# Setup of a fused layer kernel: token groups of 384, 384 and 264 in place of two of 512 and a patch, and ten identity products ahead of the first turn

## Chip, cores and metric

The kernel is one launch on one core of one Trainium2 chip. The metric is the device time of a launch in microseconds. Three runs of the kernel before gave 1665.57, 1666.29 and 1668.97 us, so the median is 1666.29 us.

## What is computed

One hybrid layer for a prompt of 1024 tokens and 8 decode tokens (1032 in all, model width 1024). What matters here is its head:

```
h    = rms_norm(x, norm_w)
proj = h @ w_in + b_in          # 1024 -> about 9,700 columns
```

The columns of `proj` then feed four branches (a gated delta rule, an RG-LRU, forgetting attention and attention to a memory), which are gated, merged and projected again. All of that is unchanged.

## The kernel before, in words

`h` is wanted transposed, with the model width on the partitions: `hH` and `hL` are [128, 8, 1032], a rounded high part and the rest, because every product of the projection is made of three passes (high weights by high `h`, high by low, low by high). A weight tile is 128 columns of `w_in`, split in the same way into `wH` (on ACT, L269, `split_hi`) and `wL` (on POOL, L276, `split_lo`). `project_step` (L335) makes one of the 8 k-steps of one tile for chosen groups of 344 tokens: three passes by up to three groups. A tile of three groups and 8 steps is 72 products. Its accumulators take three of the eight PSUM banks: tile 0 has banks 0 to 2, tile 1 has 3 to 5, and so on by turns, so that a group of a tile must not start in a bank that still holds something else.

`setup` (L357 to L586) makes `hH` and `hL` for all tokens, with tiles 0 and 1 projected in between:

- SP loads the 8 decode rows, then the 8 blocks of 128 token rows x_0 to x_7, with `norm_w` behind x_3 and the first weight tile behind x_5, then the second weight tile, then some twenty small parameter loads.
- ACT squares each block with a running sum (L448), DVE makes 1/sqrt of the sums by small dependent steps (`root`, L488 with L101 to L106, twice: for blocks 0 to 3, then for 4 to 7 and the decode rows), and the blocks are scaled by it: 0 to 3 on DVE (L494), 4 to 6 and the decode rows on ACT (L461, L465), 7 on POOL (L432).
- A "turn" (L526) is a set of PE transposes of one k of one token group into one PSUM bank, here 4 transposes of 128 columns. There are two groups of 512 tokens, so 16 turns. ACT writes the high part of a turned bank (`high`, L442), DVE the low part (`low`, L498), and the bank is free when the low part is there (`held`). The 8 decode tokens go their own way (L572, L514, L469, L518).
- PE first makes turns 0 to 5, which wait for all four scalings of DVE. Then `two_tiles` writes the order out by hand: tile 0, then tile 1, for the first 344 tokens (they need only the first token group), with the other ten turns between the steps; then tile 0 and tile 1 for the other two groups of 344, two at a time. The transposes of the parameter tables (`tables`, L531 to L536) stand behind the first step of the last loop.

The queues run in order: ACT has squares, splits, scalings and `high` in one written order, POOL has `split_lo` of tile 0, its scaling, then `split_lo` of tiles 1 and 2.

Behind it `conv_tiles` (L797) goes on with tile 2 on PE. Its own work hangs on setup's end in several chains. ACT rounds tile 2's weights once tile 0 is done, POOL makes their low part, then clears some buffers; DVE's convolution of tile 0 (L908 to L925) starts behind those, SP's loads of some narrow columns too, and SP's load of weight tile 3 stands behind these in its queue. PE's tile 3 needs tile 3's low weights, and behind its first step, before the squares' transposes (L781), it waits for the convolution of tile 0 (`fin`).

Of the kernel before, what the change touches and what calls it, by code (L numbers as in the profile page):

```python
# [356 lines left out]
def setup(K):  # L357

    nc, i, block = K.nc, K.i, K.block
    GROUPS = ((0, 1, 2, 3), (4, 5, 6, 7))  # L360
    TURNS = [(g, k) for g in range(2) for k in range(KD)]
    BANKS = [1, 2, 4, 5, 6, 7, 1, 2] + 2 * [4, 5, 6, 7]
    held = lambda x: max((y for y in range(x) if BANKS[y] == BANKS[x]), default=None)
    with ExitStack() as c:
# [4 lines left out]
        NW, HS = sb("norm_cols", [P, KD]), sb("h_sample", [P, KD, NB])  # L369
# [4 lines left out]
        made, squared, rstd = K.sem("constants_made"), K.sem("x_squared"), K.sem("x_rstd_made")  # L374
        by_act, by_dve, by_pool = (K.sem("x_scaled_" + x) for x in ("act", "dve", "pool"))
# [3 lines left out]
        sample, sampleT = K.sem("h_sample_steps"), K.sem("h_sample_turned")  # L379
# [20 lines left out]

        psum = lambda g, k: K.ps[:, BANKS[KD * g + k]]
        cols = lambda g: slice(512 * g, 512 * g + 512)
        HSP = K.ps[:, 1, 0:KD * NB]

        @block.sync
        def _(sp):
            sp.dma_start(X[0:NB, TT8], i["x_sample"][:, 0]).then_inc(x_in[TT8], 16)
            for t in range(TT8):
                sp.dma_start(X[:, t], i["x_prompt"][0, t * P:(t + 1) * P]).then_inc(x_in[t], 16)
                if t == 5:  # L410
                    K.loads(sp, 1)
                if t == 3:
                    sp.dma_start(NW[:], i["norm_w"][0].rearrange("(k p) -> p k", p=P),
                                 allow_slow_non_contiguous=True).then_inc(nw_in, 16)
            K.loads(sp, 2)
# [8 lines left out]
        def _(pool):  # L424
# [5 lines left out]
            K.split_lo(pool, 1)  # L430
            pool.wait_ge(rstd, 2)
            pool.tensor_scalar(X[:, 7], X[:, 7], RS[:, 7:8], None, ALU.mult).then_inc(by_pool, 1)  # L432
# [3 lines left out]
        def _(act):  # L436
# [7 lines left out]
            act.wait_ge(filled, 1)  # L444
            for x, t in enumerate((TT8, 0, 1, 2, 3, 4, 5, 6, 7)):
                n = P if t < TT8 else NB
                act.wait_ge(x_in[t], 16)
                act.activation(SQ[0:n], X[0:n, t], ACT.Square, accum_out=SS[0:n, t:t + 1]).then_inc(squared, 1)  # L448
                act.wait_ge(squared, x + 1)
                if t == 5:  # L450
                    K.split_hi(act, 1)
                    act.wait_ge(nw_in, 16)
                    high(0)
                    high(1)
                if t == 6:
                    high(2)
            for x in range(3, 6):
                high(x)
            act.wait_ge(rstd, 2)
            for t in (4, 5, 6):  # L460
                act.activation(X[:, t], X[:, t], ACT.Identity, scale=RS[:, t:t + 1]).then_inc(by_act, 1)  # L461
            high(6)
            high(7)
            K.split_hi(act, 2)
            act.activation(X[0:NB, TT8], X[0:NB, TT8], ACT.Identity, scale=RS[0:NB, TT8:TT8 + 1]).then_inc(by_act, 1)  # L465
            for x in range(8, 11):
                high(x)
            act.wait_ge(sample, 1)
            act.activation(K.hH[:, :, SEQ:TOK], HS[:], ACT.Identity).then_inc(sample, 1)  # L469
            for x in range(11, len(TURNS)):  # L470
                high(x)
# [12 lines left out]
        def _(dve):  # L484
            v = K.V(dve)

            def root(g, part):
# [4 lines left out]
            def scale(t):  # L492
                n = P if t < TT8 else NB
# [8 lines left out]
            dve.wait_ge(squared, 5)  # L502
            root(0, slice(0, 4))
            for t in range(4):
                scale(t)
            dve.wait_ge(nw_in, 16)
            for x, part in enumerate(TURNS):
                if x == 3:
                    dve.wait_ge(squared, 9)
                    root(1, slice(4, 9))  # L510
                low(*part)
                if x == 9:
                    dve.wait_ge(sampleT, 1)
                    dve.tensor_tensor(HS[:], HSP.rearrange("p (k b) -> p k b", b=NB),  # L514
                                      NW[:].unsqueeze(2).broadcast_to([P, KD, NB]), ALU.mult).then_inc(sample, 1)
                if x == 11:
                    dve.wait_ge(sample, 2)
# [2965 lines left out]
```

## Time and profile before

| | |
|---|---|
| runs | 1665.57, 1666.29, 1668.97 us |
| profiled execution | 1669.67 us, of which its span on the core 1668.0 us |
| mean granted TensorE clock | 0.995 |
| PE busy | 1612.3 us, 97% |
| DVE, ACT, POOL busy | 53%, 32%, 30% |

The profiled execution is one launch of its own; the span runs from its first to its last instruction. A time in the trace counts from the span's start. In a timeline row the columns are start, duration, engine, source line, operation, written<-read buffers, shapes (partitions x elements), how many instructions the row merges, and in brackets the idle time of the engine before it with what ended it.
### The profile page before, as it was taken

The numbers are of one execution on the slowest core, as the hardware profiler recorded it, in microseconds if no ns is written. First come the engines' busy times: TensorE is split into PE (matmuls) and PEld (weight loads), VectorE is DVE, ScalarE is ACT, GpSimd is POOL, SyncE is SP. The second block draws the span as 40 slices with busy tenths as digits, with TensorE's granted clock in tenths as the row PEclk, the third lists the DMA queues.
The fourth block names the chain that finished last, engine by engine and source line by source line (L and its number), as shares of the span: only waits on it lengthen the run. The fifth ranks groups of instructions, "written<-read, shape, count | busy, mean of one in ns | idle before, by whom it ended". The sixth has DMA issues, their size and how long they took to land. (4 is left out here: it accounts for less than half of the span.)

```text
span 1668.0 us, 26092 instructions
## 1 busy us (share of the span) xinstructions
PE 1612.3 (97%) x10579; PEld 1541.0 (92%) x10579; DVE 884.0 (53%) x1288; ACT 537.4 (32%) x934; POOL 502.6 (30%) x379
## 2 busy tenths in 40 slices
PE   5999999999999999999999999999999999999999
PEld 4989989999999999998889899999999999889976
DVE  4667853344444442790387672435657552995611
ACT  6323243222222222233334443321145223664200
POOL 2333415333343411911244551222212121103400
PEclk9999999999999999999999999999999999999999
DMA  4211155223222114542366352235210341535521
GB/s 156 53 26 41 44 155 135 71 71 70 71 70 71 51 49 121 149 127 63 99 191 188 104 177 107 65 115 158 71 39 14 108 109 55 164 118 152 152 77 58
DMA packets 189365, 163.16 MB, mean 98 GB/s; under 512 B 18381, under 2 KB 157056, under 8 KB 188727
## 3 DMA queue, kind: packets, MB, share of 16 engines
q1 hardware_dynamic: 189246, 161.51, 33.4%
q8 instruction: 84, 1.38, 0.4%
q14 instruction: 35, 0.28, 0.1%
HBM read 131.38 MB, written 30.22 MB: 97 GB/s over the span
## 5 line engine op out<-in xcount | busy, mean ns | idle before, releaser
L276 POOL TENSOR_TENSOR wL<-w_raw,wH 128x1024 fp32r<-128x1024 f32 (+1 forms) x112 | 238.4, 2129 | 803.1 <-ACT wH L269 803.0
L335 PE MATMUL ps<-hH,wH 128*128 128x344 f32 x1920 | 458.2, 341 | 12.6 <-PEq L196 3.6
L335 PE MATMUL ps<-hL,wH 128*128 128x344 f32 x1920 | 420.1, 321 | 0.0
L335 PE MATMUL ps<-hH,wL 128*128 128x344 f32 x1920 | 419.4, 321 | 0.0
L335 PEld LDWEIGHTS ps<-hH,wH 128*128 128x128 f32 x1920 | 316.7, 190 | 26.5 <-issue 10.7
L335 PEld LDWEIGHTS ps<-hL,wH 128*128 128x128 f32 x1920 | 327.3, 189 | 0.2
L335 PEld LDWEIGHTS ps<-hH,wL 128*128 128x128 f32 x1920 | 324.9, 189 | 0.0
L269 ACT ACTIVATE wH<-w_raw 128x1024 fp32r<-128x1024 f32 (+1 forms) x116 | 108.5, 936 | 117.6 <-PE ps L335 107.2
L2918 POOL TENSOR_SCALAR fa_logits<-fox_c_bc,token_scalars 128x128 f32<-128x128 f32 (+7 forms) x32 | 58.7, 1834 | 51.9 <-DMA fox_c_bc<-rows_g_c_beta 27.0
L1880 ACT ACTIVATE d_m<-ps 128x512 f32<-128x512 f32 x48 | 28.7, 598 | 134.8 <-PE ps L2062 134.8
L1268 DVE SCALAR_TENSOR_TENSOR m_th<-m_th,ps 128x1032 f32<-128x1032 f32 x24 | 29.5, 1228 | 61.9 <-PE ps L335 61.9
L335 PE MATMUL ps<-branch_in_r,wH 128*128 128x344 f32 x288 | 61.1, 320 | 0.0
L1950 DVE COPY_PREDICATED d_x<-dn_lo,ps 128x512 f32<-128x512 int8 x40 | 29.7, 741 | 54.8 <-PE ps L2079 54.6
L1447 DVE TENSOR_TENSOR m_th<-ps,m_th 128x512 f32<-128x512 f32 (+1 forms) x18 | 12.4, 691 | 83.4 <-PE ps L1458 83.4
L1956 DVE COPY d_y<-ps 128x512 f32<-128x512 f32 x40 | 27.6, 690 | 53.1 <-PE ps L2068 53.1
L3062 DVE SCALAR_TENSOR_TENSOR fa_logits<-ps,fox_rq,fa_logits 128x512 f32<-128x512 f32 (+3 forms) x48 | 28.0, 611 | 48.1 <-POOL fa_logits L2919 37.0
L2062 PE MATMUL ps<-d_x,d_nu 128*128 128x128 f32 x384 | 50.5, 274 | 0.0
L2062 PEld LDWEIGHTS ps<-d_x,d_nu 128*128 128x128 f32 x384 | 48.7, 191 | 0.0
L335 PEld LDWEIGHTS ps<-branch_in_r,wH 128*128 128x128 f32 x288 | 48.6, 188 | 0.0
L1273 DVE TENSOR_TENSOR merged<-merged,m_th 128x1032 f32<-128x1032 f32 x24 | 44.6, 1859 | 0.8
L3196 ACT ACTIVATE fa_pT<-ps 128x512 f32<-128x512 f32 (+3 forms) x48 | 23.5, 489 | 63.0 <-PE ps L2943 63.0
L2079 PE MATMUL ps<-d_m,d_y 128*128 128x128 f32 x320 | 42.7, 276 | 0.4
(576 smaller groups left out, 2783.9 us busy)
## 6 DMA issues: line engine op xcount, KB each, us to landing
w_raw<-in_w_in SPq DMA_DIRECT2D x80, 512.0 KB, 5.1
m_th<-gate_spill SPq DMA_DIRECT2D x28, 516.0 KB, 4.5
gate_spill<-d_gate SPq DMA_DIRECT2D x18, 516.0 KB, 3.0
fa_kv<-in_cache_fox_k SPq DMA_DIRECT2D x32, 256.0 KB, 3.1
fa_kv<-in_cache_fox_v SPq DMA_DIRECT2D x32, 256.0 KB, 3.4
w_raw<-in_w_branch SPq DMA_DIRECT2D x32, 256.0 KB, 2.9
gate_spill<-fa_gate SPq DMA_DIRECT2D x10, 516.0 KB
x_rows<-in_x_prompt SPq DMA_DIRECT2D x8, 512.0 KB, 6.3
```

The costliest lines, as they stand in the source:

```text
L269: act.activation(self.wH[:, t % 2, 0:nk], self.raw_at(t)[:, 0:nk], ACT.Identity).then_inc(self.w_hi, 1)
L276: pool.tensor_tensor(self.wL[:, t % 2, 0:nk], self.raw_at(t)[:, 0:nk], self.wH[:, t % 2, 0:nk].bitcast(F32), ALU.subtract).then_inc(self.w ...
L335: last = pe.matmul(self.ps[:, b + g, 0:cols], w[:, t % 2, k], x[:, k, g * cols:(g + 1) * cols], start=(k == 0 and n == 0), stop=(k == nk - ...
L1268: dve.scalar_tensor_tensor(o.rearrange("p (a b) -> p a b", a=3), TH[:, d % NT].rearrange("p (a b) -> p a b", a=3), 1.0, K.psum(t), ALU.add ...
L1273: dve.tensor_tensor(K.merged[:, d], K.merged[:, d], o, ALU.add).then_inc(self.summed, 1)
L1880: act.activation(M1[:], BM, ACT.Identity).then_inc(S["m1e"], 1)
L1950: dve.copy_predicated(X[:], mb(LO[:, l]), BX).then_inc(S["upx"], 1)
L1956: dve.tensor_copy(Y[:], BY).then_inc(S["upy"], 1)
L2062: last = pe.matmul(BM[:, h], NU[:, ch % 2, h], X[:, h], start=True, stop=True)
L2079: last = pe.matmul(BX[:, h], Y[:, h], M1[:, h], start=True, stop=True)
L2918: g.do(pool.tensor_scalar(lg, C[:, 0:w], K.TK[:, t, 1, h:h + 1], None, ALU.subtract))
L3062: ins = dve.scalar_tensor_tensor(lg[:, a:a + m], K.ps[:, 3 + x % 2, 0:m], rq, lg[:, a:a + m], ALU.mult, ALU.subtract)
```

## The change

Setup works in three token groups: blocks 0 to 2 (tokens 0 to 383), 3 to 5 (384 to 767), and 6, 7 with the decode rows (768 to 1031). There are 24 turns, 16 of three 128-column transposes and 8 of two and an 8-column one; the decode tokens' separate path is gone. `root` runs three times, for blocks 0 to 2, 3 to 5, and 6, 7 and decode. DVE scales blocks 0, 1, 3 and 6 and squares block 5; ACT scales 2, 4, 7 and the decode rows; POOL scales 5. The first weight tile and `norm_w` are loaded behind x_2, the second tile behind x_5. POOL splits tiles 0 and 1 before its scaling. PE makes ten products of the identity with four copies of itself (512 columns) into bank 7 before it waits for the scalings, and the three groups of 344 are projected one at a time. `K.left` no longer waits for the decode path. Declarations of buffers are left out here.

```diff
@@ -357,26 +357,27 @@
...
-    GROUPS = ((0, 1, 2, 3), (4, 5, 6, 7))
-    TURNS = [(g, k) for g in range(2) for k in range(KD)]
-    BANKS = [1, 2, 4, 5, 6, 7, 1, 2] + 2 * [4, 5, 6, 7]
+    GROUPS = ((0, 1, 2), (3, 4, 5), (6, 7, TT8))
+    TURNS = [(g, k) for g in range(3) for k in range(KD)]
+    BANKS = [1, 2, 4, 5, 6, 7, 1, 2] + 2 * [2, 5, 6, 7] + [5, 6, 7, 2, 5, 6, 7, 5]
+    AHEAD, WARM = 6, 10
     held = lambda x: max((y for y in range(x) if BANKS[y] == BANKS[x]), default=None)
@@ -398,21 +399,21 @@
...
-        psum = lambda g, k: K.ps[:, BANKS[KD * g + k]]
-        cols = lambda g: slice(512 * g, 512 * g + 512)
-        HSP = K.ps[:, 1, 0:KD * NB]
+        cols = lambda g: slice(3 * P * g, min(3 * P * (g + 1), TOK))
+        psum = lambda g, k: K.ps[:, BANKS[KD * g + k], 0:cols(g).stop - cols(g).start]
+        rows_of = lambda t: P if t < TT8 else NB
...
         @block.sync
         def _(sp):
             sp.dma_start(X[0:NB, TT8], i["x_sample"][:, 0]).then_inc(x_in[TT8], 16)
             for t in range(TT8):
                 sp.dma_start(X[:, t], i["x_prompt"][0, t * P:(t + 1) * P]).then_inc(x_in[t], 16)
-                if t == 5:
+                if t == 2:
                     K.loads(sp, 1)
-                if t == 3:
                     sp.dma_start(NW[:], i["norm_w"][0].rearrange("(k p) -> p k", p=P),
...
-            K.loads(sp, 2)
+                if t == 5:
+                    K.loads(sp, 2)
@@ -427,9 +428,9 @@
...
-            K.split_lo(pool, 1)
+            K.split_lo(pool, 2)
             pool.wait_ge(rstd, 2)
-            pool.tensor_scalar(X[:, 7], X[:, 7], RS[:, 7:8], None, ALU.mult).then_inc(by_pool, 1)
+            pool.tensor_scalar(X[:, 5], X[:, 5], RS[:, 5:6], None, ALU.mult).then_inc(by_pool, 1)
             K.split_lo(pool, 3)
...
         @block.scalar
@@ -441,33 +442,45 @@
                 act.wait_ge(xT, x + 1)
                 act.activation(K.hH[:, k, cols(g)], psum(g, k), ACT.Identity, scale=NW[:, k:k + 1]).then_inc(hi, 1)
...
-            act.wait_ge(filled, 1)
-            for x, t in enumerate((TT8, 0, 1, 2, 3, 4, 5, 6, 7)):
-                n = P if t < TT8 else NB
+            def square(t):
+                n = rows_of(t)
                 act.wait_ge(x_in[t], 16)
                 act.activation(SQ[0:n], X[0:n, t], ACT.Square, accum_out=SS[0:n, t:t + 1]).then_inc(squared, 1)
-                act.wait_ge(squared, x + 1)
-                if t == 5:
-                    K.split_hi(act, 1)
-                    act.wait_ge(nw_in, 16)
-                    high(0)
-                    high(1)
-                if t == 6:
-                    high(2)
-            for x in range(3, 6):
+                squares[0] += 1
+                act.wait_ge(squared, squares[0])
+
+            def scale(t):
+                n = rows_of(t)
+                act.activation(X[0:n, t], X[0:n, t], ACT.Identity, scale=RS[0:n, t:t + 1]).then_inc(by_act, 1)
+
+            squares = [0]
+            act.wait_ge(filled, 1)
+            for t in (TT8, 0, 1, 2):
+                square(t)
+            K.split_hi(act, 1)
+            square(3)
+            act.wait_ge(rstd, 1)
+            scale(2)
+            square(4)
+            act.wait_ge(nw_in, 16)
+            for x in range(3):
                 high(x)
+            K.split_hi(act, 2)
+            high(3)
+            high(4)
+            square(6)
+            high(5)
+            high(6)
             act.wait_ge(rstd, 2)
-            for t in (4, 5, 6):
-                act.activation(X[:, t], X[:, t], ACT.Identity, scale=RS[:, t:t + 1]).then_inc(by_act, 1)
-            high(6)
+            scale(4)
             high(7)
-            K.split_hi(act, 2)
-            act.activation(X[0:NB, TT8], X[0:NB, TT8], ACT.Identity, scale=RS[0:NB, TT8:TT8 + 1]).then_inc(by_act, 1)
-            for x in range(8, 11):
+            square(7)
+            for x in range(8, 13):
                 high(x)
-            act.wait_ge(sample, 1)
-            act.activation(K.hH[:, :, SEQ:TOK], HS[:], ACT.Identity).then_inc(sample, 1)
-            for x in range(11, len(TURNS)):
+            act.wait_ge(rstd, 3)
+            scale(7)
+            scale(TT8)
+            for x in range(13, len(TURNS)):
                 high(x)
             K.split_hi(act, 3)
@@ -484,13 +497,13 @@
         def _(dve):
...
-            def root(g, part):
+            def root(part):
                 v.do(dve.tensor_scalar(SS[:, part], SS[:, part], 1.0 / D, EPS, ALU.mult, ALU.add))
                 rsqrt(v, SS[:, part], RS[:, part], TM[:, part])
                 dve.sem_inc(rstd, 1)
...
             def scale(t):
-                n = P if t < TT8 else NB
+                n = rows_of(t)
                 dve.tensor_scalar(X[0:n, t], X[0:n, t], RS[0:n, t:t + 1], None, ALU.mult).then_inc(by_dve, 1)
...
             def low(g, k):
@@ -499,31 +512,33 @@
                                          K.hH[:, k, cols(g)].bitcast(F32), ALU.mult, ALU.subtract).then_inc(lo, 1)
...
             dve.memset(SS[:], 1.0).then_inc(filled, 1)
-            dve.wait_ge(squared, 5)
-            root(0, slice(0, 4))
-            for t in range(4):
+            dve.wait_ge(squared, 4)
+            root(slice(0, 3))
+            for t in range(2):
                 scale(t)
+            dve.wait_ge(x_in[5], 16)
+            dve.scalar_tensor_tensor(SQ2[:], X[:, 5], 1.0, X[:, 5], ALU.mult, ALU.mult,
+                                     accum_out=SS[:, 5:6]).then_inc(squared_dve, 1)
             dve.wait_ge(nw_in, 16)
             for x, part in enumerate(TURNS):
                 if x == 3:
-                    dve.wait_ge(squared, 9)
-                    root(1, slice(4, 9))
+                    dve.wait_ge(squared, 6)
+                    dve.wait_ge(squared_dve, 1)
+                    root(slice(3, 6))
+                    scale(3)
+                if x == 12:
+                    dve.wait_ge(squared, 8)
+                    root(slice(6, 9))
+                    scale(6)
                 low(*part)
-                if x == 9:
-                    dve.wait_ge(sampleT, 1)
-                    dve.tensor_tensor(HS[:], HSP.rearrange("p (k b) -> p k b", b=NB),
-                                      NW[:].unsqueeze(2).broadcast_to([P, KD, NB]), ALU.mult).then_inc(sample, 1)
-                if x == 11:
-                    dve.wait_ge(sample, 2)
-                    dve.tensor_tensor(K.hL[:, :, SEQ:TOK], HS[:], K.hH[:, :, SEQ:TOK].bitcast(F32), ALU.subtract
-                                      ).then_inc(sample, 1)
...
         def turn(pe, x):
             g, k = TURNS[x]
             if held(x) is not None:
                 pe.wait_ge(lo, held(x) + 1)
             for y, t in enumerate(GROUPS[g]):
-                last = pe.transpose(psum(g, k)[:, y * P:(y + 1) * P], X[:, t, k * P:(k + 1) * P], K.ident[:])
+                n = rows_of(t)
+                last = pe.transpose(psum(g, k)[:, y * P:y * P + n], X[0:n, t, k * P:(k + 1) * P], K.ident[0:n, 0:n])
             last.then_inc(xT, 1)
...
         def tables(pe):
@@ -537,49 +552,55 @@
...
+        def scaled(pe, g):
+
+            by = ((by_dve, 2), (by_act, 1)), ((by_dve, 3), (by_act, 2), (by_pool, 1)), ((by_dve, 4), (by_act, 4))
+            for sem, count in by[g]:
+                pe.wait_ge(sem, count)
+
         @block.tensor
         def _(pe):
             pe.wait_ge(made, 3)
-            pe.wait_ge(by_dve, 4)
-            for x in range(6):
+            for _ in range(WARM):
+                pe.matmul(K.ps[:, 7].rearrange("p (a b) -> p a b", b=P), K.ident[:],
+                          K.ident[:].unsqueeze(1).broadcast_to([P, 4, P]), start=True, stop=True)
+            scaled(pe, 0)
+            for x in range(AHEAD):
                 turn(pe, x)
...
         def left(eng):
-            eng.wait_ge(lo, 2 * KD)
+            eng.wait_ge(lo, 3 * KD)
             eng.wait_ge(tab, 4)
-            eng.wait_ge(sample, 3)
...
         def two_tiles(pe):
...
             for k in range(KD):
                 pe.wait_ge(lo, k + 1)
                 K.project_step(pe, 0, K.hH, K.hL, k, only=(0,))
-                if k < 2:
-                    turn(pe, 6 + k)
-                if k == 6:
-                    pe.wait_ge(by_act, 3)
-                    pe.wait_ge(by_pool, 1)
-                if k >= 6:
-                    turn(pe, 2 + k)
+                if AHEAD + k < KD:
+                    turn(pe, AHEAD + k)
             for k in range(KD):
                 K.project_step(pe, 1, K.hH, K.hL, k, only=(0,))
-                if k in (0, 2):
-                    turn(pe, 10 + k // 2)
-                if k == 1:
-                    pe.wait_ge(by_act, 4)
-                    pe.wait_ge(lo, 7)
-                    for q in range(KD):
-                        last = pe.transpose(HSP[:, q * NB:(q + 1) * NB], X[0:NB, TT8, q * P:(q + 1) * P],
-                                            K.ident[0:NB, 0:NB])
-                    last.then_inc(sampleT, 1)
-                if k >= 4:
-                    turn(pe, 8 + k)
-            pe.wait_ge(sample, 3)
+                if k == 0:
+                    scaled(pe, 1)
+                turn(pe, KD + k)
             for k in range(KD):
                 pe.wait_ge(lo, KD + k + 1)
-                K.project_step(pe, 0, K.hH, K.hL, k, only=(1, 2))
+                K.project_step(pe, 0, K.hH, K.hL, k, only=(1,))
+                if k == 4:
+                    scaled(pe, 2)
+                if k >= 4:
+                    turn(pe, 2 * KD + k - 4)
             for k in range(KD):
-                K.project_step(pe, 1, K.hH, K.hL, k, only=(1, 2))
+                K.project_step(pe, 1, K.hH, K.hL, k, only=(1,))
+                if k < 4:
+                    turn(pe, 2 * KD + 4 + k)
+            pe.wait_ge(lo, 2 * KD + 4)
+            for k in range(KD):
+                pe.wait_ge(lo, 2 * KD + k + 1)
+                K.project_step(pe, 0, K.hH, K.hL, k, only=(2,))
+            for k in range(KD):
+                K.project_step(pe, 1, K.hH, K.hL, k, only=(2,))
                 if k == 0:
```

## Rows read from the trace of the kernel before

**Rows 1.** The page, part 1: busy time and instructions of each engine.
```profile
PE 1612.3 (97%) x10579; PEld 1541.0 (92%) x10579; DVE 884.0 (53%) x1288; ACT 537.4 (32%) x934; POOL 502.6 (30%) x379
```

**Rows 2.** Timeline of PE, setup and the start of tile 2.
```profile
16.03 4.44 PE L526 MATMUL ps<-ident,x_rows 128*128 128x128 f32 x24 [16.03 <-DVE x_rows L494]
...
24.88 0.43 PE L335 MATMUL ps<-hH,wH 128*128 128x344 f32 x1 [2.13 <-DVE hL L498]
...
28.65 0.65 PE L335 MATMUL ps<-hH,wH 128*128 128x344 f32 x1 [1.23 <-DVE hL L498]
...
36.63 0.60 PE L526 MATMUL ps<-ident,x_rows 128*128 128x128 f32 x4
...
37.23 0.32 PE L335 MATMUL ps<-hL,wH 128*128 128x344 f32 x1
...
37.39 0.32 PE L335 MATMUL ps<-hH,wL 128*128 128x344 f32 x1
...
56.37 0.63 PE L335 MATMUL ps<-hH,wH 128*128 128x344 f32 x3
```

**Rows 3.** Stretches: busy of PE, PEld, DVE, ACT, POOL (x instructions), clock, DMA share, GB/s.
```profile
20.00:26.00 6.00, 3.87 (x28) 3.36 (x26) 4.70 (x16) 5.32 (x8) 1.93 (x1) 1.00 0.39 100
27.00:33.00 6.00, 4.77 (x19) 4.22 (x18) 2.16 (x3) 4.57 (x7) 2.37 (x1) 0.50 0.08 23
```

**Rows 4.** Timeline of ACT in setup.
```profile
8.09 1.06 ACT L448 ACTIVATE x_square<-x_rows 128x1024 f32<-128x1024 f32 x1 [0.44 <-DMA x_rows<-in_x_prompt]
...
9.47 1.06 ACT L448 ACTIVATE x_square<-x_rows 128x1024 f32<-128x1024 f32 x1 [0.23 <-DMA x_rows<-in_x_prompt]
...
14.53 1.06 ACT L269 ACTIVATE wH<-w_raw 128x1024 fp32r<-128x1024 f32 x1 [0.84 <-DMA w_raw<-in_w_in]
...
17.21 1.48 ACT L442 ACTIVATE hH<-ps,norm_cols 128x512 fp32r<-128x512 f32 x2 [1.62 <-PE ps L526]
...
24.01 3.23 ACT L461 ACTIVATE x_rows<-x_rows,x_rstd 128x1024 f32<-128x1024 f32 x3 [0.65 <-DVEq L490]
...
29.24 1.13 ACT L465 ACTIVATE x_rows<-x_rows,x_rstd 8x1024 f32<-8x1024 f32 x1
...
47.60 1.06 ACT L269 ACTIVATE wH<-w_raw 128x1024 fp32r<-128x1024 f32 x1 [6.91 <-PE ps L335]
```

**Rows 5.** Timeline of DVE in setup.
```profile
10.65 0.17 DVE L488 TENSOR_SCALAR x_ss<-x_ss 128x4 f32<-128x4 f32 x1 [9.70 <-ACT x_square L448]
...
13.14 2.74 DVE L494 TENSOR_SCALAR x_rows<-x_rows,x_rstd 128x1024 f32<-128x1024 f32 x4
...
24.07 2.07 DVE L498 SCALAR_TENSOR_TENSOR hL<-ps,norm_cols,hH 128x512 fp32r<-128x512 f32 x3 [0.15 <-DVE x_rstd L106]
```

**Rows 6.** Timeline of POOL: its scaling in setup, then low weights of tiles 2 and 3.
```profile
24.07 2.85 POOL L432 TENSOR_SCALAR x_rows<-x_rows,x_rstd 128x1024 f32<-128x1024 f32 x1 [5.97 <-DVEq L490]
...
48.74 2.37 POOL L276 TENSOR_TENSOR wL<-w_raw,wH 128x1024 fp32r<-128x1024 f32 x1 [16.96 <-ACT wH L269]
...
62.09 2.40 POOL L276 TENSOR_TENSOR wL<-w_raw,wH 128x1024 fp32r<-128x1024 f32 x1 [7.45 <-ACT wH L269]
```

**Rows 7.** Timelines of POOL and of DVE around 215 us.
```profile
214.66 2.36 POOL L276 TENSOR_TENSOR wL<-w_raw,wH 128x1024 fp32r<-128x1024 f32 x1 [7.34 <-ACT wH L269]
...
214.69 2.35 DVE L106 SCALAR_TENSOR_TENSOR y_rs<-y_tm,y_rs 128x2 f32<-128x2 f32 x1
```

**Rows 8.** Groups of PE by shape: busy, mean ns of one, idle before.
```profile
L2956 PE MATMUL ps<-fox_v_rows,fa_pT 128*128 128x128 f32 x288 | 40.1, 275 | 0.0
...
L2934 PE MATMUL ps<-merged 128*128 128x512 f32 x48 | 24.2, 600 | 2.1 <-DVE fa_logits L3062 2.1
```

**Rows 9.** Timelines behind setup: ACT, DVE and PE.
```profile
60.88 1.06 ACT L269 ACTIVATE wH<-w_raw 128x1024 fp32r<-128x1024 f32 x1 [1.42 <-DMA w_raw<-in_w_in]
...
65.63 1.22 DVE L925 SCALAR_TENSOR_TENSOR branch_in<-ca_th,branch_in 128x1032 f32<-128x1032 f32 x1
...
69.16 0.60 PE L781 MATMUL ps<-ident,branch_in 128*128 128x128 f32 x4
```

More of the change, by code:

```diff
@@ L368, in setup @@
         SS, RS, TM = sb("x_ss", [P, 9]), sb("x_rstd", [P, 9]), sb("x_tm", [P, 9])
-        NW, HS = sb("norm_cols", [P, KD]), sb("h_sample", [P, KD, NB])
+        NW, SQ2 = sb("norm_cols", [P, KD]), sb("x_square_dve", [P, D])
         BR, PR = sb("bias_rows", [NBROW, P]), sb("par_rows", [NPROW, P])
@@ L374, in setup @@
         made, squared, rstd = K.sem("constants_made"), K.sem("x_squared"), K.sem("x_rstd_made")
+        squared_dve = K.sem("x_squared_dve")
         by_act, by_dve, by_pool = (K.sem("x_scaled_" + x) for x in ("act", "dve", "pool"))
@@ L378, in setup @@
         xT, hi, lo = K.sem("x_transposed"), K.sem("h_hi"), K.sem("h_lo")
-        sample, sampleT = K.sem("h_sample_steps"), K.sem("h_sample_turned")
         par_dmas = []
```

## The prediction

> **What bounds the kernel now.** I read the page's busy times first: PE is busy for 1612.3 of 1668.0 us [rows 1], so only idle or slow PE time can be won, and 16 us of its 56 idle ones stand before the first turn. Next, PE's timeline. The first turn starts at 16.03, when DVE has scaled; PE then stands for 2.13 us before 24.88 and 1.23 before 28.65, both times for a low part, and tile 2 starts at 56.37 [rows 2]. From there its products stand shoulder to shoulder (tile 3's first extra work at 69.16 has no wait) [rows 9], so setup's worth is read at 56.37. Third, the clock: 1.00 granted from 20 to 26, 0.50 from 27 to 33 [rows 3], so after the first of these gaps PE dropped to 1.2 GHz. The 24 first transposes took 4.44 us, 0.18 each, where four took 0.44 later (36.63 to 37.39 less two products of 0.16) [rows 2]: the first turns too ran mostly at the lower clock. Start, two gaps, slow clock: that is all the change can reach.
>
> PE's work itself hardly changes: 144 products of 0.158 us, and 16 turns of 0.33 plus 8 of about 0.3 in place of 16 of 0.44 and eight 8-column ones.
>
> **Loads and the first scalings.** x_2 landed at about 8.05, x_3 at 9.4 (squares at 8.09 and 9.47), the first weight tile at 14.5, 2.0 behind x_5 [rows 4]. Behind x_2 it lands at about 10.1; x_3 then at 11.6, x_5 at 14.4. The total is the same, SP issues the same instructions, and the second weight tile lands near 16, before it is wanted. ACT has squared decode, 0, 1, 2 at 9.25 and rounds the weights from 10.1 to 11.15. DVE's `root` takes 2.34 us, and scalings start 2.49 after its start (10.65 to 13.14) [rows 5]: 9.27 gives 11.76. Alone, two DVE scalings of 0.68 (2.74 for four) [rows 5] end at 13.2; ACT, behind x_3's square (11.65 to 12.8), has scaled x_2 at 13.95 (1.14 each, 3.23 for three) [rows 4]. Naively the first turn would start at 14.1, 1.9 earlier.
>
> **What meets what.** POOL makes `wL` from 11.2 to 13.6 (2.36 to 2.42 us) [rows 6, 7], on top of `root` and scalings; before, it came when DVE had finished. Elsewhere in this kernel POOL's `wL` started at 214.66 and a DVE step of the same rsqrt, 128x2, started 0.03 us later: it took 2.35 us instead of 0.16 and ended with POOL's [rows 7]. A `root` step reads two buffers in SBUF; `low` reads PSUM and one buffer, and three of them beside POOL's scaling took their usual 0.69 [rows 5, 6]. So I take: POOL's `wL` holds up `root`, fully. Bounds: nothing, if the steps slip by, and 2.4 us each time. I take 2.3, the row being of the same code. `root` then has its last two steps behind POOL, ends at 13.85, DVE's two scalings end at 15.4, ACT's at 15.1. First turn at 15.6: 0.4 us won, not 1.9.
>
> The Trainium skill, SBUF — State Buffer, section "Who interferes with whom", says a DVE instruction with two SBUF inputs contends with a GpSimd instruction that reads SBUF, and that a `tensor_scalar` in a 2-port mode does too. By it the scalings are held as well as `root`; the start would be 15.6 in either reading.
>
> **The ten products.** Price: a 512-column fp32 product lasts 600 ns where a 128-column one lasts 275 [rows 8], so 384 more columns cost 0.325 and the pitch is about 0.43 at 2.4 GHz, 0.86 at 1.2. The constants are ready at 1.6; ten products end between 6 and 10.2. They delay nothing. Nor do I think they help: PE then idles for over 5 us, and the clock had dropped here behind a gap of 2.13 us and thin work [rows 2, 3]. Bounds: nothing, and 1.9 us (18 transposes at 0.107 instead of 0.213) at the front, of which almost all is lost at the next wait, below; 0.15 would reach it.
>
> The Trainium skill's page TensorE: Matmul & The Clock Gate, section "Why this matters for your kernels", advises matmuls ahead of the work as a warm-up; by it the products would bring the 1.9. Its Part 4 says that transposes do not raise the clock; this trace disagrees: PE had nothing but transposes until 20.2, and from 20 to 26 the granted clock is 1.00 [rows 3].
>
> **Second group.** Turns at 1.2 GHz: 0.64 each from 15.6. ACT's `high` follows a turn by 0.33 (16.03 plus four slow transposes, to 17.21) [rows 2, 4] and takes 0.56 for 384 columns (0.69 for 512): 16.6, 17.2, 17.85. DVE squares x_5 in about 1.3 from 15.4 (1.28 is what other two-input steps of 1024 columns take, an estimate from 1.22 for 1032 [rows 9]) and makes three `low` until 19.0. Then `root` 2. But ACT rounds tile 1 right behind `high` 2, 18.4 to 19.4, and POOL's second `wL` runs from 19.5 to 21.9: three steps of `root` are done, nine wait. It ends at 23.5. Block 3 is scaled at 24.4, the fourth low part is there at 24.9, PE goes on at 25.0. PE has done six turns (19.4), three steps and turns 6 and 7 (21.5) by then: a gap of 3.5 us, longer than the 2.13 before. Without the hold-up it goes on at 21.4.
>
> From there five low parts come every 0.52, then tile 1's first group has eight steps of 0.47 with a turn of 0.33 each: 33.8. POOL's scaling of x_5 (23.65 or 24.4, 2.85 long [rows 6]) is done before PE wants it at 28. For the clock I add 1.7: before, six microseconds at 0.50 [rows 3] cost half of the work in them, 3; here low parts pace half of that stretch. Turn 15 ends at 35.5.
>
> **Third group, a new wait.** `low` 11 ends at 33.8, `root` 3 (POOL idle) at 36.15; ACT then scales x_7 and, as dear with 8 rows, the decode rows (1.13) [rows 4]: 38.45. `high` 13 stands behind these, `low` 13 ends at 39.5, and turn 16 needs its bank. PE reaches that point at 38.1: 1.5 us of stall, turn 16 at 39.6. From there PE has 5.0 + 2.6 + 3.8 + 5.1 = 16.5 us of its own: (tile 1 group 2 with four turns; the rest of tile 0 group 2; tile 0's last group; tile 1's with 1.35 for the tables). Tile 2 starts at 56.1, against 56.37: **0.3 won**.
>
> **Behind setup.** The chains that start when tile 0 is complete keep their length, but PE reaches tile 2 sooner after it: 5.1 us instead of 8.9 (47.5 to 56.37) [rows 2, 4], since only one group of tile 1 is left. Tile 2's low weights come 3.6 after that point (48.74 + 2.37) [rows 6]: in time. Tile 3's come 17.0 after it (62.09 + 2.40; ACT waited for the load at 60.88) [rows 6, 9]; PE, with 11.4 for tile 2, is there at 16.5 and waits 0.6. One step later it wants DVE's finished tile 0, 19.4 after that point (65.63 + 1.22); PE is there at 18.6, where before it came at 69.16, 2.3 late [rows 9]: another 0.9. Behind that DVE has slack again. **1.5 given back.**
>
> **Sum.** -0.3 + 1.5 = +1.2 us. The profiled execution took 1669.67 (span 1668.0 and 1.67 around it) and would take 1670.9; it lies 3.4 above the median, so the forecast is 1666.29 + 1.2 = **1667.5 us**.
>
> **Rivals.** *POOL's low weights leave `root` alone* (or land in its gaps, or the loads shift them off): first turn at 14.2, PE goes on after step three at 21.4 behind a gap of 1.1, no clock drop, so 3.6 and 1.7 earlier than above: tile 2 at 50.8, 5.6 won, 1.5 given back, 1662.2. For it: the clash was seen once on such a step. Against: that once was total. Chance 0.2.
>
> *The slower end: POOL's scaling beats DVE's scaling of block 3.* Both wait for `root` 2; before, POOL and DVE's next instruction both started at 24.07, 0.15 behind it [rows 5, 6]. If POOL's 2.85 goes first and holds block 3's scaling, the fourth low part is 2.8 later, PE's gap is over 6 us and the slow clock sure: 1667.5 + 2.7 = 1670.2. It decides within about 0.01 us. Chance 0.2, with a slow clock of 6 us instead of 3 (another 1.7 to 2) counted beside it. The Trainium skill's page SBUF — State Buffer, in the same section, says that whoever issues first holds the shared ports for the whole instruction; no row here shows it for these two forms.
>
> *The change does not do what it says: the clock stays up from the ten products to the first turn.* That gives 0.15, then the gap of 3.5 us comes all the same: 1667.3. Chance 0.05.
>
> The forecast itself has 0.45 (1665.5 to 1669.5: clock cost between nothing and 3), and 0.1 is left for what I did not see.
>
> **Numbers.** 0.2% is 3.3 us, about what a measurement of this kernel tells from no change. Faster by more needs the first rival (0.2); slower by more the second, or a clock that stays down longer (0.25); within 0.2% is 0.55. Range: 1662.0 to 1671.5, from the first rival to the second with 1.3 on top.
>
> **What would show it.** DVE `root` steps of over 1 us beside POOL's L276, twice; first turn near 15.6 (wrong if 14.1); low clock in the first turns; a PE gap near 21 to 25 with a low clock behind it; a gap near 38 for `low`; tile 2 near 56; gaps of 0.6 and 0.9 in tile 3. If no `root` step is longer than 0.2, the forecast falls to the first rival.

## The result, and the profile after

The changed kernel takes 1670.20 us (median of 22 runs, 1666.37 to 1673.67), the kernel before, run beside it, 1666.39 (22 runs, 1663.03 to 1672.09). The medians are 3.8 us apart; over all runs the ratio is 1.0019, with a 95% interval of 1.001 to 1.0027, which is 3.2 us slower (1.7 to 4.5). The forecast was +1.2.

PE's timeline of the changed kernel (columns as in [rows 2]):

```profile
1.64 10.24 PE L565 MATMUL ps<-ident 128*128 128x512 f32 x20 [1.64 <-POOL ones L430]
15.65 4.10 PE L541 MATMUL ps<-ident,x_rows 128*128 128x128 f32 x18 [3.77 <-DVE x_rows L507]
...
24.94 0.66 PE L335 MATMUL ps<-hH,wH 128*128 128x344 f32 x1 [2.22 <-DVE hL L511]
...
39.40 0.56 PE L541 MATMUL ps<-ident,x_rows 128*128 128x128 f32 x3 [1.32 <-DVE hL L511]
...
40.47 0.53 PE L541 MATMUL ps<-ident,x_rows 128*128 128x128 f32 x3
...
41.51 0.54 PE L541 MATMUL ps<-ident,x_rows 128*128 128x128 f32 x3
...
58.20 0.64 PE L335 MATMUL ps<-hH,wH 128*128 128x344 f32 x3
...
72.44 0.66 PE L802 MATMUL ps<-ident,branch_in 128*128 128x128 f32 x4 [0.94 <-DVE branch_in L946]
```

Against [rows 2]: the first turn is 0.4 us earlier, the second gap of before (1.23) is gone, a new one (1.32) stands before turn 16, and tile 2 starts 1.83 us later. In tile 3 PE waits 0.94 us where it never waited before. In the third group a step with its turn takes 1.04 us (40.47 to 41.51).

DVE's timeline, a step of `root` 1 and of `root` 2, and POOL's beside them:

```profile
11.30 2.33 DVE L104 TENSOR_TENSOR x_tm<-x_rstd 128x3 f32<-128x3 f32 x1
...
19.62 2.25 DVE L104 TENSOR_TENSOR x_tm<-x_rstd 128x3 f32<-128x3 f32 x1
...
23.60 0.75 DVE L507 TENSOR_SCALAR x_rows<-x_rows,x_rstd 128x1024 f32<-128x1024 f32 x1
...
11.27 2.35 POOL L276 TENSOR_TENSOR wL<-w_raw,wH 128x1024 fp32r<-128x1024 f32 x1 [9.68 <-ACT wH L269]
19.47 2.38 POOL L276 TENSOR_TENSOR wL<-w_raw,wH 128x1024 fp32r<-128x1024 f32 x1 [5.86 <-ACT wH L269]
23.61 3.38 POOL L433 TENSOR_SCALAR x_rows<-x_rows,x_rstd 128x1024 f32<-128x1024 f32 x1 [1.76 <-DVEq L503]
```

One 3-column step in each of these two `root`s ends with POOL's low weights; its neighbours take 0.16 to 0.17. The last row is the race for block 3: DVE's scaling went first and took its usual 0.75, POOL's took 3.38 instead of 2.85 [rows 6].

The same hold-up stands behind the wait of 0.94 in tile 3, where the prediction did not look for it. In the chain of tile 0 that PE waits for, an 8-column step that takes 0.22 elsewhere took 2.36 beside POOL's low weights of tile 3 (DVE's and POOL's timelines):

```profile
67.42 2.36 DVE L939 SCALAR_TENSOR_TENSOR branch_in<-dn_conv_states,half_par,branch_in 128x8 f32<-128x8 f32 x1
```
```profile
67.27 2.49 POOL L276 TENSOR_TENSOR wL<-w_raw,wH 128x1024 fp32r<-128x1024 f32 x1 [7.14 <-ACT wH L269]
```

The kernel before has it too, beside its low weights at 62.09 [rows 6]; its neighbours take 1.28:

```profile
62.19 3.38 DVE L917 SCALAR_TENSOR_TENSOR branch_in<-ca_in,half_par,branch_in 128x1024 f32<-128x1024 f32 x1
```

Where the 3.2 us are: PE starts tile 4 at 83.30; before it was 79.97, so 3.3 later. That is about the measured difference. The two profiled executions do not show it at their ends (1668.42 after, 1669.67 before), because of a stretch further on, where one execution of the two lost time. ACT's rounding of a later weight tile, before and then after (this view: ACT's timeline):

```profile
150.43 1.06 ACT L269 ACTIVATE wH<-w_raw 128x1024 fp32r<-128x1024 f32 x1 [5.04 <-DMA w_raw<-in_w_in]
```
```profile
150.01 1.06 ACT L269 ACTIVATE wH<-w_raw 128x1024 fp32r<-128x1024 f32 x1 [1.30 <-DMA w_raw<-in_w_in]
```

Before, ACT was there 3.3 us sooner, but the load landed no sooner. SP issues it behind eight small stores, and these took 10.1 us in the profiled execution before and 3.7 in that after:

```profile
129.99 10.10 SPq L225 DMA_DIRECT2D out_fox_logf<-s_values  x8
```
```profile
133.58 3.68 SPq L225 DMA_DIRECT2D out_fox_logf<-s_values  x8
```

The stores are not the whole reason. The load was issued at 140.87 before and at 141.72 after, and took 10.1 us to land against 8.7 (medians of its two halves); in the run without products, below, the stores took 9.2 us, the load landed in 7.2, and PE did not wait. Before, PE then waited 2.65 us at 152 and ran 3.4 us at 0.50 granted; after, it did neither. From there on the profiled execution after is the earlier one. Single launches of one kernel differ by 7 to 9 us, so below the stages are read from the traces and the times from many runs.

### The profile page after: what moved, and what is told of

Read it like the earlier page. It is cut to its first block and busy times, and to the rows that moved or that the text cites. A ratio compares the mean times of both kernels' runs of the same rounds, so it can differ in the third digit from the quotient of the medians.

```text
span 1666.7 us, 26157 instructions
## 1 busy us (share of the span) xinstructions
PE 1623.3 (97%) x10599; PEld 1544.6 (93%) x10599; DVE 894.6 (54%) x1308; ACT 538.1 (32%) x939; POOL 507.3 (30%) x379
## 5 line engine op out<-in xcount | busy, mean ns | idle before, releaser
L2939 POOL TENSOR_SCALAR fa_logits<-fox_c_bc,token_scalars 128x128 f32<-128x128 f32 (+7 forms) x32 | 58.7, 1833 | 52.0 <-DMA fox_c_bc<-rows_g_c_beta 26.8
```

The costliest lines, as they stand in the source:

```text
L2939: g.do(pool.tensor_scalar(lg, C[:, 0:w], K.TK[:, t, 1, h:h + 1], None, ALU.subtract))
```

## The experiments

All ratios are against the kernel before, run on the same chip. "Tile 2" and "tile 4" are the starts of PE's first product of that tile; the changed kernel has 58.20 and 83.30, the kernel before 56.37 and 79.97.

**Without the products.**

```diff
-    AHEAD, WARM = 6, 10
+    AHEAD, WARM = 6, 0
```

> The changed kernel without its ten products. My theory: they neither help nor harm beyond the state of the clock; the first turn still starts at 15.6 to 15.7, the clock is low in the first turns up to about 19, PE goes on after step three at 24.9 as before, tile 2 starts within 0.5 us of the changed kernel's 58.2, and the time is the same within 0.2%. Rival (the products pay, as a warm-up should): tile 2 starts 1.9 us later than 58.2 or more. Second rival (the products harm, since they raise the clock early and it falls again just before the first turn): tile 2 is over 1 us earlier.

Ratio 1.0019 (1.0006 to 1.0032), as with them. First turn at 14.93, PE goes on at 24.20, tile 2 at 57.63. The shift of 0.6 to 0.7 is there from the first turn on. In this execution x_2 landed earlier (ACT squares it at 7.67, in the changed kernel at 8.34), so `root` 1 was over before POOL could hold it, and POOL held up DVE's scaling instead. DVE's timeline:

```profile
11.35 3.48 DVE L507 TENSOR_SCALAR x_rows<-x_rows,x_rstd 128x1024 f32<-128x1024 f32 x2 [0.15 <-DVE x_rstd L106]
...
18.87 2.27 DVE L104 TENSOR_TENSOR x_tm<-x_rstd 128x3 f32<-128x3 f32 x1
```

Two scalings take 1.42 us alone, so a scaling is held like a `root` step. POOL's low weights end at 13.61 here and at 13.62 in the changed kernel. There two steps of `root` and both scalings still stood behind that and ended at 15.60; here only the scalings did, and ended at 14.83, which is the 0.7. That the products have no part in when x_2 lands is taken, not shown: it is one trace of each. Neither rival holds.

**POOL's low weights off both roots.**

```diff
-            K.split_lo(pool, 2)
+            pool.wait_ge(by_dve, 2)
+            K.split_lo(pool, 1)
             pool.wait_ge(rstd, 2)
```

> POOL waits with tile 0's low weights for DVE's two scalings, and makes tile 1's behind its own scaling, so that no low weights run beside a root. My theory (POOL's low weights hold up root): every root step takes 0.16 to 0.17, first turn at 14.3 instead of 15.65, root 2 is over at 21.0 instead of 23.45, PE goes on after step three at 22.5 instead of 24.94; then tile 1 waits for its low weights until about 27.0 (before: 28.95), so tile 2 starts at 56.2 instead of 58.2, less if the clock stays up. Rival (DVE would be late in any case, through block 5's load or square): PE goes on at 24.5 or later and tile 2 starts at 58.

No `root` step is over 0.17 us. PE's timeline:

```profile
14.17 3.02 PE L542 MATMUL ps<-ident,x_rows 128*128 128x128 f32 x18 [2.00 <-ACT x_rows L455]
...
22.36 0.42 PE L335 MATMUL ps<-hH,wH 128*128 128x344 f32 x1 [1.92 <-DVE hL L512]
...
26.78 0.43 PE L335 MATMUL ps<-hH,wH 128*128 128x344 f32 x1 [1.58 <-POOL wL L276]
...
60.36 0.64 PE L335 MATMUL ps<-hH,wH 128*128 128x344 f32 x3
```

First turn 14.17 (expected 14.3), PE goes on at 22.36 (22.5), tile 1 at 26.8 (27.0): the hold-up cost 1.5 us at the front and 2.6 at the second group. The rival falls. It did not go altogether: POOL's low weights now met DVE's square of block 5, which took 2.75 us instead of 1.22, and PE waited 0.43 for the first low part behind it. But tile 2 came at 60.36, not 56.2, in this execution. The reason is the clock, in the stretches 18 to 39 and 40 to 49 (columns as in [rows 3]):

```profile
18.00:39.00 21.00, 16.18 (x103) 14.28 (x103) 13.69 (x42) 12.59 (x23) 5.70 (x2) 0.98 0.23 59
40.00:49.00 9.00, 9.00 (x32) 6.85 (x30) 2.46 (x5) 2.40 (x5) 0.00 (x0) 0.50 0.00 0
```

After the gap of 1.3 us at 37, the third group, with its steps and turns, ran at 1.2 GHz. The ratio over all runs is 1.0023 (1.0004 to 1.0042), so the gain was not kept. This execution (1678.29 us, mean clock 0.989) is one of three slow ones of the twelve (1675 to 1680 us, 0.988 to 0.991). The other nine have 0.994 to 0.999 and a mean of 1667.3, against 1665.5 for the kernel before: so the low clock of this trace is not what most runs show, and even they are not faster than the kernel before. Leaving the three out is a choice made after the runs, so these means only hint.

**Whole-block transposes for the decode tokens.** The decode block is cleared by POOL, loaded behind x_2, squared behind x_7, and transposed like the others:

```diff
-                last = pe.transpose(psum(g, k)[:, y * P:y * P + n], X[0:n, t, k * P:(k + 1) * P], K.ident[0:n, 0:n])
+                last = pe.transpose(K.ps[:, BANKS[x], y * P:(y + 1) * P], X[:, t, k * P:(k + 1) * P], K.ident[:])
```

> The decode block is cleared first and transposed with all 128 rows and columns, as the others are; its load and square come later. Theory (the 8-row transposes of the third group cost more than their 0.08 each, because PE changes between 128 rows and 8 and back in every turn): a third-group step with its turn takes 0.80 instead of 1.04, eight of them 2 us, tile 2 starts at 56.2. Rival (the third group's turns are slow for another reason, the wait for banks or low parts): step with turn still 1.04, tile 2 at 58.2 or later.

PE's timeline:

```profile
40.10 0.49 PE L543 MATMUL ps<-ident,x_rows 128*128 128x128 f32 x3
...
40.90 0.49 PE L543 MATMUL ps<-ident,x_rows 128*128 128x128 f32 x3
...
56.17 0.64 PE L335 MATMUL ps<-hH,wH 128*128 128x344 f32 x3
```

A step with its turn takes 0.80, tile 2 starts at 56.17: 2.0 us, as expected, of which 1.9 lie behind turn 16 (39.27 to 56.17, against 39.40 to 58.20). By the difference of the two steps, a transpose of 8 rows between others of 128 costs PE about 0.35 us (0.24 more than the 0.107 of a whole one), though it passes a sixteenth of the columns. The run shows the cost; that PE's change between 128 rows and 8 is the reason is not shown. Ratio 1.0015 (1.0002 to 1.0029): too wide to show the 2 us by itself.

**Root 3 in DVE's idle time.**

```diff
-                if x == 12:
+                if x == 8:
                     dve.wait_ge(squared, 8)
...
-            for x in range(8, 13):
-                high(x)
+            high(8)
             act.wait_ge(rstd, 3)
             scale(7)
+            high(9)
+            high(10)
             scale(TT8)
-            for x in range(13, len(TURNS)):
+            for x in range(11, len(TURNS)):
                 high(x)
```

> Root 3 and block 6's scaling move ahead of low 8, where DVE stands idle, and ACT's scalings of block 7 and decode stand between high 8 and high 11. Theory: the gap of 1.3 us before turn 16 goes and nothing takes its place; tile 2 starts at 56.9. Rival: the moved scalings hold up high 9 to 11, so that a gap opens before turn 12 or 13, and tile 2 stays near 58.

The gap before turn 16 is gone, none has opened, and tile 2 starts at 56.98 though the first turn came 0.47 later than in the changed kernel. Ratio 1.0004 (0.9989 to 1.002), so the time shows neither a gain on the changed kernel nor a difference from the kernel before.

**Both together.**

> The changed kernel with the whole-block decode transposes and the early root 3 together. If the two costs are separate, they add: tile 2 starts at 58.2 - 2.0 - 1.3 = 54.9; tile 4 starts 25.1 later, at 80.0, where the kernel before has 79.97, so the time is that of the kernel before (ratio 0.999 to 1.001). Rival (both are one wait seen from two sides): tile 2 at 56 or later, ratio 1.001 or more.

Tile 2 at 55.35, tile 4 at 80.45. The clock was at 0.50 for 6.8 us from 23.7 here, against 3.4 in the changed kernel; that is the likely reason for the 0.45 missing at both tiles. Within that the costs add in the trace. Ratio 1.001 (0.9995 to 1.0025), inside the forecast, but also compatible with the rival's.

**All three repairs.** POOL's wait for DVE's two scalings, `split_lo(pool, 2)` behind it, and in ACT's queue:

```diff
+            K.split_hi(act, 2)
             act.wait_ge(nw_in, 16)
-            for x in range(3):
+            for x in range(4):
                 high(x)
-            K.split_hi(act, 2)
-            high(3)
```

> The same, and POOL's low weights kept off the roots: tile 0's wait for DVE's two scalings, tile 1's are asked for before high 0, beside DVE's low parts, which read PSUM. Theory: first turn at 14.2, at most one short hold-up at the start of root 2, which ends at 22.1 instead of 23.45; PE goes on after step three at 23.5 instead of 24.94; tile 2 at 53.5, tile 4 at 78.6, so 1.3 us under the kernel before, less if the clock falls for longer. Rival (low parts are held up by POOL too): PE goes on at 24.9 or later.

PE's timeline:

```profile
14.47 2.16 PE L544 MATMUL ps<-ident,x_rows 128*128 128x128 f32 x18 [1.83 <-ACT x_rows L457]
18.62 0.43 PE L335 MATMUL ps<-hH,wH 128*128 128x344 f32 x1 [1.99 <-DVE hL L515]
...
23.50 0.65 PE L335 MATMUL ps<-hH,wH 128*128 128x344 f32 x1 [1.53 <-DVE hL L515]
...
52.99 0.64 PE L335 MATMUL ps<-hH,wH 128*128 128x344 f32 x3
```

PE goes on at 23.50, tile 2 at 52.99, tile 4 at 78.08. Ratio 0.9983 (0.9969 to 0.9996): just clear of the kernel before, and clear of the changed kernel's 1.0019. Against the run with both other repairs, which differs in nothing but this order and was measured beside the same runs of the kernel before, the median falls from 1667.78 to 1663.86 us (12 runs each): this pair shows the price of POOL's hold-up in the time itself. Low parts beside POOL's low weights took their usual time; the rival falls. The order has a price that the forecast left out. ACT now rounds tile 1 ahead of `high` 0 and waits 0.93 us there for that tile's load, and DVE's square of block 5 took 2.30 us beside POOL's low weights of tile 0.

**The kernel before with the ten products.** The same loop of ten products ahead of PE's wait for DVE's scalings, and nothing else.

> The kernel before with the ten products alone. Theory: they end near 12, the clock falls again before or in the first turns at 16.0; tile 2 starts within 1.7 us of 56.37 either way, by where the clock's rise and fall come to lie, and the time is the same within 0.2%. Rival (products are a warm-up): first 24 transposes in 2.6 us instead of 4.4 and tile 2 at 54.6.

Here the forecast of the clock was wrong, while that of the time held. The products lasted until 13.56, the clock stayed up, and the 24 transposes took 2.84 us instead of 4.44:

```profile
15.92 2.84 PE L526 MATMUL ps<-ident,x_rows 128*128 128x128 f32 x24 [2.37 <-DVE x_rows L494]
...
24.11 0.43 PE L335 MATMUL ps<-hH,wH 128*128 128x344 f32 x1 [2.20 <-DVE hL L498]
...
55.37 0.64 PE L335 MATMUL ps<-hH,wH 128*128 128x344 f32 x3
```

Tile 2 is 1.0 earlier, not 1.8, since PE meets the same waits for low parts sooner; ratio 0.9998 (0.9983 to 1.0013).

**Fourteen products.**

```diff
-    AHEAD, WARM = 6, 10
+    AHEAD, WARM = 6, 14
```

> The changed kernel with fourteen products, which end near 15.3, just before the first turn. Theory: the first 18 transposes now take about 2.0 us instead of 3.8, and nothing comes of it, because the fourth low part is still at 24.9: the gap before step three's successor grows from 2.2 to about 5 us, the clock falls in it, and tile 2 starts at 58 to 60. Rival (the clock at the front is what holds the start back): PE goes on at 23 and tile 2 starts at 56.3.

```profile
15.51 2.13 PE L541 MATMUL ps<-ident,x_rows 128*128 128x128 f32 x18
...
24.42 0.66 PE L335 MATMUL ps<-hH,wH 128*128 128x344 f32 x1 [4.56 <-DVE hL L511]
...
58.24 0.64 PE L335 MATMUL ps<-hH,wH 128*128 128x344 f32 x3
```

The turns are done 2 us sooner, and the gap behind them is 2.3 longer. Tile 2 at 58.24, ratio 1.0017 (1.0 to 1.0034): nothing won. This is the clearest of the runs on the products: the rival's 23 and 56.3 did not come.

**The squares' transposes one step later**, on top of all three repairs:

```diff
-                        if 3 <= j < squares + 3 and k in (0, 3):
-                            if k == 0:
+                        if 3 <= j < squares + 3 and k in (1, 4):
+                            if k == 1:
```

> The kernel with all three repairs, and the squares' transposes of each tile (with the wait for DVE's finished tile) behind its second and fifth step instead of its first and fourth. Theory (the gap of 0.94 us in tile 3 is PE being early by less than one step of 1.42): no gap in tile 3, tile 4 starts 24.1 us after tile 2 instead of 25.1, so about 0.9 us faster than without it. Rival (the gap moves on to a later wait, since DVE's chain is what bounds here): tile 4 still 25.0 after tile 2, or a new gap before 120 us.

No gap in tile 3; tile 2 at 52.12, tile 4 at 76.07, 23.95 apart. Ratio 0.9989 (0.9975 to 1.0003), not told apart from that without it.

**Identity products in PE's gaps.**

```diff
             for x in range(AHEAD):
                 turn(pe, x)
+            fill(pe, 2)
...
+                if k == 3:
+                    fill(pe, 2)
                 pe.wait_ge(lo, k + 1)
```

> The same with two identity products behind turn 5 and two ahead of the wait of step 3, into bank 3, which tile 1 starts later. Theory (the low clock from 19.7 to 26.5 costs PE time behind the wait of step 3, and work in the gaps keeps it up): granted clock 1.00 from the first turns on, PE goes on at 23.5 as before, tile 1's first step at 26.4 instead of 27.3, tile 2 at 52.1 instead of 53.0. Rival (the fill stands in the way where DVE is early, or nothing is won since low parts pace this stretch): tile 2 at 53.0 or later.

The clock stayed up through setup:

```profile
14.00:20.00 6.00, 4.63 (x27) 3.31 (x28) 4.19 (x5) 3.97 (x8) 3.77 (x2) 1.00 0.84 278
20.00:26.00 6.00, 5.18 (x27) 3.64 (x26) 5.47 (x19) 5.66 (x10) 3.63 (x2) 1.00 0.57 147
```

Yet tile 2 starts at 52.97 in this execution, 0.85 later than in the run with the squares' transposes one step later. The whole 0.85 is there at PE's first step (19.25 for 18.40), and does not come from the fill: ACT waited longer for tile 1's load ahead of `high` 0. ACT's timeline, that run's row and then this one's:

```profile
16.08 1.06 ACT L269 ACTIVATE wH<-w_raw 128x1024 fp32r<-128x1024 f32 x1 [0.95 <-DMA w_raw<-in_w_in]
```
```profile
16.93 1.06 ACT L269 ACTIVATE wH<-w_raw 128x1024 fp32r<-128x1024 f32 x1 [2.03 <-DMA w_raw<-in_w_in]
```

The wait for the fourth low part ended at 24.12 for 23.28, and from there tile 2 is 28.85 us away here and 28.84 there, where the clock had been low from 15.5 to 22.3. So the higher clock ahead of that wait bought nothing in these two traces. The ratio is the best of all, 0.9973 (0.9959 to 0.9986), 4.5 us under the kernel before; whether the fill has a part in it is open, since the interval overlaps those of the other three kernels that have all the repairs.

**The same without any products ahead.** `WARM` is 0, the squares' transposes stay one step later, nothing fills the gaps.

> The kernel of c1 without its ten products. Theory: they are worth only what the place of the clock's fall makes of them: first turn at 14.3, PE goes on after step three at 23.5, tile 2 within 1 us of c1's, time the same within 0.1 to 0.2%. Rival (with the start no longer held up, a warm start pays): tile 2 over 1.5 us later than with the products.

The first turn came at 14.86 (expected 14.3), PE goes on at 23.76, tile 2 at 52.60, 0.5 behind; ratio 0.998 (0.9966 to 0.9995). The rival falls.

## Why the prediction was right, point by point

- *POOL's low weights hold up `root`.* Right, twice, with 2.33 and 2.25 us; first turn 15.65 for 15.6, PE goes on at 24.94 for 25.0. The run with POOL's weights off the roots has 14.17 and 22.36. The step that took the price from one row of another stage decided the forecast's sign: without it the prediction had 1662.2. Its sentence that the start would be 15.6 "in either reading" was not right. When POOL held the scalings and not `root`, the first turn came at 14.93. And the first rival priced the hold-up too high: it put tile 2 5.3 us earlier, where the two runs with and without it, 55.35 and 52.99, are 2.4 apart, since the weights then stand in the way elsewhere.
- *The race for block 3.* DVE won by 0.01 us, as taken; that rival did not come. In all eleven traces with the new groups DVE's scaling took 0.75 or 0.76 and POOL's 3.38 or 3.39 instead of 2.85, with the starts at most 0.01 us apart: the one that went first kept its time.
- *The ten products delay nothing and bring nothing.* The time says so (1.0019 with and without). Their length was mis-sized: a product is two instructions, 20 in 10.24 us, and they ended at 11.9 instead of 10.2 at most. That the clock is down in the first turns held in the changed kernel's trace, but not when the products were put into the kernel before, nor in two runs of the new groups with the same ten (18 transposes in 2.83 and 2.16 us instead of 4.10): that rival, given 0.05, was more likely than that. It was cheap for the reason given, the next wait takes it back (fourteen products: 2 us sooner, 2.3 longer gap).
- *The gap before 24.94.* It was 2.22 us and not 3.5. The clock was at 0.50 from 14.7 to 21.5, and the prediction had priced only the six turns at that clock, not the three steps and two turns behind them. The end of the gap is DVE's, so this changed nothing behind it.
- *Transposes and the clock.* The prediction took it from [rows 3] that transposes alone raised the clock. That row does not carry it, since the same view has 1.00 from 16 to 18 us too, where a transpose took 0.21 us. The pitch does: from 19.04 on ten transposes took 1.18 us, with nothing but transposes before them.
- *Clock behind the gap.* 1.7 was added; it was low from 24.95 to 28.37, and the first 344 tokens of both tiles and turn 15 were done at 35.3 for 35.5.
- *Third group, new wait.* 1.32 for 1.5, turn 16 at 39.40 for 39.6.
- *"8 of about 0.3" was the term that was mis-sized.* From turn 16 on PE needed 18.8 us, not 16.5: eight turns with an 8-row transpose cost 0.57 each. No row of an 8-row transpose among full ones stood behind the 0.3. Whole blocks take 1.9 of it away. It is why tile 2 came at 58.2 and not at 56.1, and why the forecast was 2 us short.
- *Behind setup, 1.5 given back.* Tile 4 starts 25.1 us after tile 2 (23.6 before): 1.5. In tile 3 itself PE waited 0.24 and 0.94, for 0.6 and 0.9. The chain's length of 19.4 us, taken over from the kernel before, holds 2.1 us of POOL's hold-up in both kernels. By an estimate from the rows above, DVE would be done at 70.25 without it, and PE gets there at 71.5, so the second wait would be gone; no run moved POOL's weights there. One step's delay of the squares' transposes brings 0.9 to 1.1 of the 1.5 back (tile 4 is 23.95 to 24.15 us behind tile 2 in the three runs that have it).

The range held the result, and the most likely class (within 0.2%) holds its ratio, by a hair, which is luck: the interval reaches to 1.0027, and the medians alone give 0.23%. The slower side had its share for other mechanisms than the one that came. The direction rests on two terms that were measured as forecast, the hold-up and the time given back; the size was 2 us short.

## What to carry to other kernels

Before work is moved between VectorE and GpSimd, lay their timelines on top of each other: a chain of tiny dependent VectorE steps is as exposed to a long GpSimd instruction as a large one. Here an order of ACT's queue that moved that instruction beside PSUM-reading work removed the clash; it cost a wait for a load, and was worth it. A transpose of a few rows is not priced by its size when it stands between full ones. And a stage that ends sooner for PE shortens the cover of the chains that start at its end, so look one tile further before counting a gain.

## What was not expected of the hardware

- An 8-row transpose among 128-row ones: about 0.35 us, against 0.107 for a full one. Eight of them in a row had taken 0.66 together in the kernel before (PE's timeline):

```profile
34.09 0.66 PE L572 MATMUL ps<-ident,x_rows 8*128 8x8 f32 x8
```
- POOL's low weights hold steps of DVE with one input in SBUF as well: both scalings (3.48 us for two instead of 1.42), and in the run of both together a 3-column step of `root` 2 with one input (L102, 2.27 instead of 0.17). A longer step that starts beside POOL's instruction takes its own time and most of what is left of POOL's: the square of block 5 took 2.17 to 2.76 us instead of 1.22.
- A 512-column fp32 product counts as two instructions of about 0.43 us each at the full clock; 28 took 14.03 us.
- The clock fell to 1.2 GHz for 10.2 us in the third group of one execution (39.2 to 49.4), with PE's records busy throughout that stretch, behind a gap of only 1.3 us; in others with the same gap it did not.
- Eight small stores took 10.1 us to issue in one execution and 3.7 in another (5.8 and 9.2 in two more), and the weight load behind them took 7.2 to 10.1 us to land. Together these moved PE by 4.4 us between the two profiled executions: at 145 us the changed kernel was 3.3 behind, at 161 it was 1.1 ahead.
